# Two adaLN products moved into the drain of the prompt attention, squares put ahead of row copies, and constants put first on the sync queue

## The reference

```python
for layer in range(2):
    sh, sc, gt = split(silu(c) @ ada_mix_w[layer] + ada_mix_b[layer], 3)
    h = rms_norm(x, g_pre_mix[layer]) * (1 + sc) + sh
    mix = multiscale_pool(h) if layer == 0 else dilated_attention(h, w_q, w_o, shared K/V)
    x = x + gt * rms_norm(mix, g_post_mix[layer])
    sh, sc, gt = split(silu(c) @ ada_ffn_w[layer] + ada_ffn_b[layer], 3)
    h = rms_norm(x, g_pre_ffn[layer]) * (1 + sc) + sh
    f = swiglu(h) if layer == 0 else top-2-of-8 experts(h)
    x = x + gt * rms_norm(f, g_post_ffn[layer])
    if layer == 0: K, V = rope/split(rms_norm(x, g_kv) @ w_kv)      # shared by layer 1
```

## Time and profile before

| | |
|---|---|
| median of 3 runs | 1710.91 us (1709.56 to 1714.78) |
| the profiled execution | 1712.1 us, of which the span from first to last instruction is 1709.9 us |
| mean granted TensorE clock | 0.959 of 2.4 GHz |
| busy in the span | PE 1590.5 us (93%), PEld 1298.5 (76%), DVE 1251.6 (73%), ACT 982.3 (57%), POOL 155.9 (9%) |
| moved by DMA | 512.28 MB, mean 300 GB/s |

### The profile page before, as it was taken

One profiled execution on the slowest core, in us unless ns is written; L12 is line 12 of the kernel. 1 busy time (PEld: TensorE's weight loads), 2 busy tenths in 40 slices (PEclk: granted clock), 3 DMA queues, 4 the chain that ended last, 5 costly groups with the idle time before them and its releaser, 6 DMA issues.

```text
span 1709.9 us, 22933 instructions
## 1 busy us (share of the span) xinstructions
PE 1590.5 (93%) x8697; PEld 1298.5 (76%) x8697; DVE 1251.6 (73%) x1097; ACT 982.3 (57%) x885; POOL 155.9 (9%) x135
## 2 busy tenths in 40 slices
PE   6889999799899768799999999999999999999996
PEld 3579999598785545378888888888888888888874
DVE  4454543668782543568888898888888888889996
ACT  2344432433332432367777777877777877777774
POOL 0000000026540421200000000000000000000310
PEclk9899999899899879699999999999999999999998
DMA  9895544945468127869999999999999999999991
GB/s 345 320 336 174 183 157 154 339 153 197 160 223 307 61 74 262 293 245 379 370 389 380 362 391 376 367 393 378 368 381 373 377 385 368 383 370 370 395 392 54
DMA packets 248253, 512.28 MB, mean 300 GB/s; under 512 B 9045, under 2 KB 68613, under 8 KB 248175
## 3 DMA queue, kind: packets, MB, share of 16 engines
q1 hardware_dynamic: 241015, 490.27, 79.9%
q0 software_dynamic: 4768, 16.89, 2.5%
q10 hardware_dynamic: 2400, 4.17, 0.7%
HBM read 498.19 MB, written 13.82 MB: 299 GB/s over the span
## 4 chain that ended last, share of the span: by engine, by line
PE 76%; DVE 10%; DMA 5%; POOL 3%; issue 3%; ACT 2%; SPq 1%; DVEq 0%; ACTq 0%; POOLq 0%
PE wide L474 22%; PE wide L475 22%; PE wide L476 22%; DVE w_lo L1729 2%; POOL phase L1907 2%; DMA ring<-in_ada_mix_w 2%; DVE phase L1570 2%; DMA ring<-in_ada_ffn_w 1%; PE wide L930 1%; POOL phase L1913 1%; ACT w_hi L1262 1%; PE wide L536 1%; PE wide L525 1%; SPq L437 1%; DMA ring<-in_cache_v 1%
## 5 line engine op out<-in xcount | busy, mean ns | idle before, releaser
L1729 DVE TENSOR_TENSOR w_lo<-ring,w_hi 128x2048 fp32r<-128x2048 f32 x336 | 767.7, 2290 | 113.7 <-ACT w_hi L1262 112.3
L1262 ACT ACTIVATE w_hi<-ring 128x2048 fp32r<-128x2048 f32 x336 | 643.6, 1919 | 216.1 <-PE wide L476 214.4
L474 PE MATMUL wide<-w_hi,xe_hi 128*128 128x512 f32 x896 | 355.7, 397 | 5.6 <-DVE w_lo L1729 3.0
L475 PE MATMUL wide<-w_lo,xe_hi 128*128 128x512 f32 x896 | 350.2, 391 | 0.0
L476 PE MATMUL wide<-w_hi,xe_lo 128*128 128x512 f32 x896 | 350.1, 391 | 0.0
L404 DVE TENSOR_TENSOR w_lo<-ring,w_hi 128x2048 fp32r<-128x2048 f32 (+1 forms) x58 | 139.1, 2400 | 109.5 <-ACT w_hi L1002 109.2
L474 PE MATMUL wide<-tHi,w_hi 128*128 128x264 f32 x672 | 198.5, 295 | 20.4 <-DVE mLo L1488 20.4
L475 PE MATMUL wide<-mLo,w_hi 128*128 128x264 f32 x736 | 212.1, 288 | 0.0
L474 PEld LDWEIGHTS wide<-w_hi,xe_hi 128*128 128x128 f32 x896 | 168.9, 188 | 45.2 <-DVE w_lo L1729 8.6
L476 PEld LDWEIGHTS wide<-w_hi,xe_lo 128*128 128x128 f32 x896 | 168.8, 188 | 35.8
L475 PEld LDWEIGHTS wide<-w_lo,xe_hi 128*128 128x128 f32 x896 | 169.0, 189 | 33.4
(11 more groups left out here) (307 smaller groups left out, 1719.1 us busy)
## 6 DMA issues: line engine op xcount, KB each, us to landing
ring<-in_moe_w SPq DMA_DIRECT2D x336, 1024.0 KB, 7.7
ring<-in_ffn_w SPq DMA_DIRECT2D x30, 1024.0 KB, 5.4
ring<-in_ada_mix_w SPq DMA_DIRECT2D x24, 1024.0 KB, 8.9
ring<-in_ada_ffn_w SPq DMA_DIRECT2D x24, 1024.0 KB, 12.0
ring<-in_w_q SPq DMA_DIRECT2D x12, 1024.0 KB, 9.3
ring<-in_cache_k SPq DMA_DIRECT2D x24, 512.0 KB, 4.9
ring<-in_cache_v SPq DMA_DIRECT2D x24, 512.0 KB, 6.2
ring<-in_w_kv SPq DMA_DIRECT2D x8, 1024.0 KB, 6.4
```

Source lines behind the costliest of these rows:

```text
L474: pe.matmul(out, a[0], b[0], start=start, stop=False, skip_group_check=True)
L475: pe.matmul(out, a[0], b[1], start=False, stop=False, skip_group_check=True)
L1262: act.activation(w_hi[:, (NSPLIT + k) % PAIRS, :], ring[:, slot, :], ACT.Copy).then_inc(hi_done, 1)
L1729: dve.tensor_tensor(w_lo[:, i, :], ring[:, slot, :], w_hi[:, i, :].bitcast(F32), ALU.subtract).then_inc(lo_done, 1)
```

## The change

Five edits:

1. The two loads of the constants go from ACT's DMA queue to the head of SP's.
2. In set 1, `ada_product(1, 0)` goes ahead of the pool mixer and norm 1, with its row copy on ACT, and norm 2 comes after product 2 instead of product 1.
3. In set 2, ACT does the squares of norm 3 ahead of the row copy of step 0.
4. Products 0 and 1 of set 3 go into the last two turns of the prompt attention, into banks 0 and 1 instead of 2 and 3, without the columns; their row copies go with them on ACT, and their columns go behind the first two products of `w_o`.
5. The rest of set 3 starts with product 2. Norm 5 comes after it, norm 6 after product 3 (they stood after products 0 and 2), and the squares of norm 5 go ahead of the row copy.

```diff
@@ block.sync
+            sp.dma_start(const[:, CNT:IOTA_KEPT], ...).then_inc(in_const, 16)
+            sp.dma_start(const[:, IOTA_KEPT:NCONST - IOTA_LEFT], ...).then_inc(in_const, 16)
             sp.dma_start(xtok[:, 0:2, :], ...).then_inc(in_x, 16)
@@ block.tensor
-            def ada_product(s, j):
+            def ada_product(s, j, columns=True):
...
-                out = bank[2 + j % 2]
+                out = bank[j if (s == 3 and j < 2) else 2 + j % 2]
...
-                if j >= 1:
+                if j >= 1 and columns:
                     ada_columns(s, j - 1)
...
             ada_columns(0, 5)
-            pool_mixer()
-            norm_sum(1)
             for j in range(6):
                 ada_product(1, j)
-                if j == 1:
+                if j == 0:
+                    pool_mixer()
+                    norm_sum(1)
+                if j == 2:
                     norm_sum(2)
...
                 if 2 <= p < KC + 2:
                     weights_to_columns(p - 2, 1)
+                if p == KC + 1:
+                    ada_product(3, 1, columns=False)
                 if 1 <= p < KC:
                     score_step(p, 1)
                 if p >= 2:
                     values(p - 2)
                 if 1 <= p <= KC:
                     weights_to_columns(p - 1, 0)
+                if p == KC:
+                    pe.wait_ge(a_exp, 4 * KC)
+                    ada_product(3, 0, columns=False)
...
                 mm.then_inc(pair_used, 1)
+                if c < 2:
+                    ada_columns(3, c)
             pe.wait_ge(wo_taken, KC)
-            for j in range(6):
-                ada_product(3, j)
-                if j == 0:
+            for j in range(2, 6):
+                ada_product(3, j, columns=(j > 2))
+                if j == 2:
                     norm_sum(5)
-                if j == 2:
+                if j == 3:
                     norm_sum(6)
             ada_columns(3, 5)
@@ block.scalar
-                act.activation(arow[:, j % 2, :], bank[2 + j % 2][:, :], ACT.Copy).then_inc(arow_ready, 1)
-
-            act.dma_start(const[:, CNT:IOTA_KEPT], ...).then_inc(in_const, 16)
+                act.activation(arow[:, j % 2, :], bank[j if (s == 3 and j < 2) else 2 + j % 2][:, :], ACT.Copy).then_inc(arow_ready, 1)
...
-            act.dma_start(const[:, IOTA_KEPT:NCONST - IOTA_LEFT], ...).then_inc(in_const, 16)
...
-            for hf in range(2):
-                pool_out(range(KC)[HALVES[hf]])
-                squares(1, mT, hf)
-            root(1)
-            pool_state_out()
             for j in range(6):
                 ada_rows(1, j)
-                if j == 1:
+                if j == 0:
+                    for hf in range(2):
+                        pool_out(range(KC)[HALVES[hf]])
+                        squares(1, mT, hf)
+                    root(1)
+                    pool_state_out()
+                if j == 2:
                     norm(2, xT)
...
+            for hf in range(2):
+                squares(3, mT, hf)
             for j in range(6):
                 ada_rows(2, j)
                 if j == 0:
-                    norm(3, mT)
+                    root(3)
...
                     highs(i_wo + p - 4)
+                if p == KC:
+                    ada_rows(3, 0)
             values_high(KC - 1)
+            ada_rows(3, 1)
...
-            for j in range(6):
+            for hf in range(2):
+                squares(5, woT, hf)
+            ada_rows(3, 2)
+            root(5)
+            ada_rows(3, 3)
+            norm(6, xT)
+            for j in range(4, 6):
                 ada_rows(3, j)
-                if j == 0:
-                    norm(5, woT)
-                if j == 2:
-                    norm(6, xT)
```

More of the change, by code:

```diff
@@ L411, in _ @@
         def _(sp):
+            sp.dma_start(const[:, CNT:IOTA_KEPT], w["shape_constants"][:, CNT:IOTA_KEPT]).then_inc(in_const, 16)
+            sp.dma_start(const[:, IOTA_KEPT:NCONST - IOTA_LEFT], w["shape_constants"][:, IOTA_KEPT + IOTA_LEFT:NCONST]).then_inc(in_const, 16)
             sp.dma_start(xtok[:, 0:2, :], w["x_prompt"][0].rearrange("(c p) d -> p c d", p=P)).then_inc(in_x, 16)
@@ L1014, in ada_rows @@
                     act.wait_ge(ada_turned, 6 * s + j - 1)
-                act.activation(arow[:, j % 2, :], bank[2 + j % 2][:, :], ACT.Copy).then_inc(arow_ready, 1)
-            act.dma_start(const[:, CNT:IOTA_KEPT], w["shape_constants"][:, CNT:IOTA_KEPT]).then_inc(in_const, 16)
+                act.activation(arow[:, j % 2, :], bank[j if (s == 3 and j < 2) else 2 + j % 2][:, :], ACT.Copy).then_inc(arow_ready, 1)
             act.dma_start(crow[0:1, :], w["c_prompt"]).then_inc(in_c, 16)
             act.dma_start(crow[1:9, :], w["c_sample"]).then_inc(in_c, 16)
-            act.dma_start(const[:, IOTA_KEPT:NCONST - IOTA_LEFT], w["shape_constants"][:, IOTA_KEPT + IOTA_LEFT:NCONST]).then_inc(in_const, 16)
             act.dma_start(vrow1[0:48, :], w["ada_mix_b"].rearrange("l (m p) -> (l m) p", p=P)).then_inc(in_vec, 16)
```

## The result

The changed kernel takes 1698.98 us (median of 5 runs, 1697.78 to 1703.08) against 1711.38 (5 runs, 1709.56 to 1714.78): ratio 0.9923, 95% interval 0.9909 to 0.9936, so 12.4 us by the medians and 11 to 16 by the interval. The forecast was 1701, with its own range 1699 to 1703.5, at whose lower end the median lies; with the rivals the range was 1697.5 to 1706. The profiled execution has a span of 1696.7 us, against 1709.9.

The account below looks back on a forecast made before the run. PE was taken to bound the kernel, chiefly in the expert loop, which passes earlier savings on. Terms 2.2 + 1.7 + 9.5 - 3.4 = 10.0 us off 1710.9 gave 1701 us, range 1699 to 1703.5, with rivals 1697.5 to 1706.

Parts of the forecast that it names:

- The bound: Expert loop: PE bounds it and the diff leaves it alone, so a microsecond saved before it shortens the end equally.
- Constants: Start of the kernel: constant loads ahead on SP delay prompt and slabs by up to 1.3 us; 0.5 was taken.
- Set 1: Second adaLN set: mixer 1.6 us late, but three products instead of four after the second sum; 2.2 us gained.
- Squares of norm 3: Set 2: PE's wait of 1.69 us before the sum goes; 1.7 us gained (1.4 to 1.8).
- The drain: End of prompt attention: two products make `w_o` start 1.5 us late; with their columns PE leaves it 3.4 late.
- The 1.9 for the columns: Inside `w_o`: columns of two products cost 0.97 us each, 1.9 together, undiminished because PE bounds `w_o`.
- Set 3: Fourth adaLN set, after `w_o`: 24.4 us to `ada_take` instead of 33.92, no DMA ending it; 9.5 us saved.
- The third rival: Set 3 still hidden behind its loads: last slab held until about E+27, saving 3.9, 1706.5 us; chance 0.07.
- PE's gap before norm 6: Set 3: PE idles some 3.3 us before the second sum, whose slow first half adds 0.8 us.
- stay at half clock: Rival, end of prompt attention: both products cost 7.8 us at half clock, gain 5.8, 1705 us; chance 0.17.
- the low clock: Rival: half clock lasts into `w_o`, making the kernel slower, up to 24 us lost and 1725 us; chance 0.03.
- the rival's 1.3: Rival: start slips by all of 1.3 us, mixer 3.1 late, second set gains nothing, 1703 us; chance 0.18.

Follow-up runs that it names:

- e11_norm2_only: The kernel before with only norm 2 moved behind product (1,2), product (1,0) staying behind the pool mixer: 1715.91 us, ratio 1.0019.
- e8_hole: The changed kernel with products (3,0) and (3,1) both put ahead of values(6), where PE waits for DVE: 1698.25 us, ratio to before 0.9916.
- e5_order_only: The changed kernel without products in the prompt attention's last turns, all six products of set 3 standing behind `w_o`: 1705.93 us, ratio to before 0.9965.
- e7_fill_gap: The changed kernel with product (3,4) moved ahead of the sum of norm 6: 1697.49 us, ratio to before 0.9906.
- e12_after_again: The changed kernel itself, unaltered, measured once more on the same chip as its neighbouring runs: 1697.80 us, ratio to before 0.9913.

## Why the prediction was right, and where it was not

**The bound.** Right: experts and tail took the same time from `ada_take(3)` on, and all but 0.6 us of the gain was won ahead of it.

**Constants.** Mis-sized: -0.5 forecast, -1.55 measured in the mean. The step that failed is "If the other loads fill those first moments nothing is lost"; they don't: the DMA engines run half empty for some 2.5 us, and 0.54 MB is missing in the end. That the full 1.3 us were at stake had been seen. The Trainium skill (DMA: Bandwidth & Descriptors, "Issuing engines are not separate DMA queues") says that a second issuing engine saves sequencer time alone. By it the move was priced at 1.3, and the runs agree with that price more than with the one taken. They go somewhat beyond it: the two issues took 0.83 us on SP and the first slab was issued 0.96 later, yet the bytes lost are worth 1.4.

**Set 1.** Right in sign, mis-sized (2.2 forecast, 3.57 measured in the first profile; 4.4 without the slip by the table, where 2.7 stood), and wrong in its cause. Two sentences fail. "The weight stream runs at 386 GB/s without a break": the row was of 48 to 50, and 18 us later the stream stood. "So the slots of the last two slabs come free before the second sum": true, and worth nothing by itself, as `e11_norm2_only` shows. The gain needs product (1,0) ahead of the mixer, which the prediction booked only as a cost of 1.6. As a cost it was in fact 2.3 at the mixer's start and only 0.5 at the sum of norm 1 (66.03 against 65.54), because the mixer ran at the full clock from its start (granted 1.00 from 54 to 58, against 0.50 before). Product (1,0) alone, with norm 2 left behind (1,1), was not run, so how much of the 4.4 needs both halves stays open.

**Squares of norm 3.** Right: 1.5 against 1.7, no gap before the sum.

**The drain.** Right in its mechanism: 2.85 and 1.92 for the two products, full clock by the second, `w_o` entered 1.4 us late where 1.5 was forecast (0.9 to 1.5 in the five profiles with the edit). Mis-sized in the sum: E is 1.5 late in the mean, not 3.4. The 1.9 for the columns was added to a `w_o` that would still start slow; but PE comes to it at the full clock now, and with the columns inside it `w_o` takes 25.95 us in all five, only 0.3 more than the 25.7 (24.9 to 26.1) of the six without. `e8_hole` shows the other side: free products, and a `w_o` that starts at half clock again.

**Set 3.** Right in its mechanism, 8.4 against 9.5. The loads ended this stage and don't any more; `e5_order_only` shows that without the products in the drain they would have, to the tenth (33.89 against 33.92). The third rival, that they still would, did not come. The term that was too small is PE's gap before norm 6: priced at 0.8 for a sum slow in its first half, it was slow throughout, 6.70 us against 4.65, 2.05 in all; `e7_fill_gap` gets it back. The Trainium skill (TensorE: Matmul & The Clock Gate, "Why this matters for your kernels") advises against long idle gaps of PE between bursts of matmuls. The runs agree: 2.9 us for one product put into the gap of 3.40.

**The rivals.** The drain did not stay at half clock, and the low clock did not last into `w_o`. Set 1 did not lose its gain: the start lost about the rival's 1.3 (1.18 in the first profile, 1.55 in the mean), and product (1,0) did run at half clock in four profiles (3.64 us for it in `e12_after_again`), but take 0 to take 1 was 36.8 to 37.9 in these four, against 41.64 without the edit.

That the total came out 2 us from the forecast is partly luck: the errors by place are -1.05, +1.7, -0.2, +1.9 and -1.1, and add to +1.2. The first pair of profiles differs by 13.2 us; 0.9 of it lies in the stretch that no edit touches and 0.6 behind take 3, and the forecast has neither.

## What to carry to other kernels

Where weights come through a ring of slots, look along the whole stage for stretches in which the stream stands because no consumer releases a slot; here one product moved ahead of such a stretch, with the norm behind it, was worth more than its own time, and reordering behind it was worth nothing. Read the stream's rate over every stretch before calling it unbroken. A stage that overlaps with nothing can be shortened by work from the next one, but put it into an idle gap, and see what clock PE then has at the next dense stage.

## What the runs showed of the hardware that was not expected

- Two small loads ahead of the large ones on one queue cost more than their issue times (0.83 us): the DMA engines stood half empty for some 2.5 us, and 5.48 MB instead of 6.02 were moved in 20 us, worth 1.4 us.
- The clock of a sum went with the gap ahead of it: after 3.40 us of idleness the 16 matmuls took 6.70 us in the changed kernel (granted 0.50) and 5.62 to 6.75 in the five others with that gap; with gaps of 0.55 and 0.65 us in its place each half took 2.05 (granted 1.00).
- A stage that no edit touches, from set 2 to the end of the prompt attention, varies by 5 us between profiles of nearly equal kernels, and with it the granted clock, from 0.93 to 0.91. What sets it stays open.
